# A three-block network on one core: row chains moved beside projections, narrow columns in one piece, eleven early expert picks

## What is computed (the reference, cut to what matters)

```
# block 1, end: product-key experts (peer); per token 8 heads x 16 picks = 128 experts
q = hb @ w_q                                   # 1024 -> 2048
s = q . sub_keys ; sub_s, sub_i = top_k(s, 16) # two half keys per head
top_s, top_i = top_k(sub_s0 + sub_s1, 16)      # 16 of 256 sums
act = gelu(hb . expert_u[expert]) * softmax(top_s)
out = sum over the 128 picks of act * expert_v[expert]
# block 2, two linear-attention branches in front of a scan over time
gla:  log_a = -softplus(-(lr @ w2 + b2)) / 16           ; cum = cumsum per chunk
hgrn: log_a = logaddexp(log lb, log(1-lb) + logsigmoid(f)); cum = cumsum per chunk
      k = (1 - lb) * sigmoid(-f) ; q = silu(q) * 128 ** -0.5
# block 3, two branches with one rate per head and token
mlstm: F = cumsum(logsigmoid(f + fb)) ; running maximum of i + ib - F
mamba: dt = softplus(dt + bias) ; cs = cumsum(-exp(a_log) * dt)
```

## Time and profile before

| | |
|---|---|
| median of 3 runs | 4499.88 (4499.08 to 4502.44) |
| profiled execution | 4488.02, span of the core 4486.3 |
| TensorE busy / VectorE busy | 83% / 65% of the span |
| ScalarE busy / GpSimd busy | 19% / 20% |
| granted TensorE clock, mean over the span | 0.943 |
| DMA | 900.51 MB, mean 201 GB/s, of which 656.07 MB in the software queue |

### The profile page before, as it was taken

How to read it: one execution, slowest core, us unless ns; L and a number is a source line. 1 busy time by engine, 2 the same in 40 slices (tenths; PEclk the granted TensorE clock), 3 DMA queues, 4 the chain that set the end, 5 groups by cost and what they waited for, 6 DMA issues and landing times. The chain is left out here.

```text
span 4486.3 us, 42942 instructions
## 1 busy us (share of the span) xinstructions
PE 3731.5 (83%) x15030; PEld 2541.7 (57%) x15030; DVE 2931.1 (65%) x5200; ACT 834.7 (19%) x1667; POOL 883.9 (20%) x810
## 2 busy tenths in 40 slices
PE   4999988778778777767999795959938997998987
PEld 3777774223222222225688685736726775777865
DVE  6653667787877878666555557638855546565774
ACT  1111111111111111111211225217721202311000
POOL 2010014344343434331000000025630000001001
PEclk8999999999999999998999897979968998999998
DMA  5523227999999999972234220339932131122321
GB/s 211 181 84 102 100 85 323 423 424 423 424 423 414 419 417 413 417 297 90 85 127 140 82 90 10 104 116 381 387 110 76 43 95 57 43 94 76 102 72 71
DMA packets 201760, 900.51 MB, mean 201 GB/s; under 512 B 21202, under 2 KB 23011, under 8 KB 122339
## 3 DMA queue, kind: packets, MB, share of 16 engines
q0 software_dynamic: 90448, 656.07, 35.9%
q1 hardware_dynamic: 105680, 230.81, 15.4%
q10 hardware_dynamic: 5428, 11.04, 0.7%
HBM read 869.03 MB, written 40.89 MB: 203 GB/s over the span
## 5 line engine op out<-in xcount | busy, mean ns | idle before, releaser
L123 DVE CAST ring_high<-ring_raw 128x2048 fp32r<-128x2048 f32 (+3 forms) x184 | 212.0, 1152 | 618.8 <-PE psum L153 521.5
L1395 PE MATMUL psum<-slots_ring,evacuation_tmp 128*128 128x512 f32 x816 | 404.2, 618 | 103.3 <-DVE evacuation_tmp L1489 102.7
L151 PE MATMUL psum<-ring_high,h_features 128*128 128x512 f32 x1120 | 452.8, 404 | 19.8 <-PEq L50 12.1
L153 PE MATMUL psum<-ring_high,h_features 128*128 128x512 f32 x1120 | 442.6, 395 | 0.0
L152 PE MATMUL psum<-ring_low,h_features 128*128 128x512 f32 x1120 | 442.5, 395 | 0.0
L125 DVE TENSOR_TENSOR ring_low<-ring_raw,ring_high 128x2048 fp32r<-128x2048 f32 (+3 forms) x184 | 394.6, 2144 | 15.2 <-issue 1.3
L151 PE MATMUL psum<-h_features,ring_high 128*128 128x512 f32 (+4 forms) x920 | 365.9, 398 | 30.9 <-DVE ring_low L125 17.3
L1395 PE MATMUL psum<-slots_features,evacuation_tmp 128*128 128x512 f32 x612 | 302.1, 617 | 78.2 <-DVE evacuation_tmp L1489 78.1
L152 PE MATMUL psum<-h_features,ring_high 128*128 128x512 f32 (+4 forms) x920 | 362.6, 394 | 0.0
L153 PE MATMUL psum<-h_features,ring_low 128*128 128x512 f32 (+4 forms) x920 | 362.0, 393 | 0.0
L1395 PEld LDWEIGHTS psum<-slots_ring,evacuation_tmp 128*128 128x128 f32 x816 | 138.2, 189 | 368.4 <-DVE evacuation_tmp L1489 269.3
(11 more groups left out here) (580 smaller groups left out, 6965.3 us busy)
## 6 DMA issues: line engine op xcount, KB each, us to landing
ring_raw<-in_w_in SPq DMA_DIRECT2D x94, 1024.0 KB, 5.2
ring_raw<-in_w_up_pairs SPq DMA_DIRECT2D x20, 1024.0 KB, 5.0
ada_ring<-in_w_ada POOLq DMA_DIRECT2D x16, 1024.0 KB, 5.7
ring_raw<-in_w_out SPq DMA_DIRECT2D x12, 1024.0 KB, 5.1
moe_entries<-in_const_zero_rows POOLq DMA_DIRECT2D x23, 512.0 KB, 4.1
row_room<-moe_entries SPq DMA_DIRECT2D x23, 512.0 KB
moe_results<-rows_out SPq DMA_DIRECT2D x23, 512.0 KB, 9.1
ring_raw<-in_w_down SPq DMA_DIRECT2D x10, 1024.0 KB, 4.9
```

Of the source, the lines that this page charges most:

```text
L123: nc.vector.tensor_copy(high, whole)
L151: nc.tensor.matmul(out, a[0], b[0], start=start, stop=False)
L153: return nc.tensor.matmul(out, a[1], b[0], start=False, stop=stop)
L1395: mm = nc.tensor.matmul(banks(t)[q], diagonal[:, n % DIAGONALS, :], slots[slot_of[n]][:, D + q * BANK:D + (q + 1) * BANK], start=i == 0, s ...
```

## The change

Five parts.

1. `peer`: 12 slots instead of 10 (two lie in the ring's raw places, so this stage no longer loads pieces for the next one; `norm` with rows does it instead). Eleven picks can be issued before `projected`: picks 0 to 2 at once, 3 when the last piece of half 0 is split, 4 to 6 into the slots of 0 to 2 when these were taken, 7 when the last piece of half 1 is split, 8 to 10 when TensorE has used the last half 0. VectorE makes the dot products of the first seven during the projection and adds them itself (`sum_early`), without TensorE. The key scores of a unit are issued one group after its projection, and the split pieces and routing steps are in another order.
2. GLA: the small matmul goes to the head of the `gdn_out` projection, and the rest of the chain beside it (`gla_decay`).
3. HGRN: bounds, sigmoid and silu go into the side of `gla_gates` (`hgrn_bound`), soft maxima and sums beside the `gla_out` projection (`hgrn_decay`).
4. mLSTM and Mamba: `mif` and `sdt` become one piece `few3` of 80 columns, projected first in `mlstm_in` as one group; both row chains run beside the rest of that projection (`rate_rows`). One stage (`turn_rows`) transposes all four rows. Mamba's chain is gone from its place.
5. `few` of block 2 becomes one piece of 80 columns and one group of 24 matmuls.

The diff, cut to its core:

```diff
+            if aside_pe is not None:
+                aside_pe(pe, lambda t: bank(1 - base % 2, t), *aside_sems)
...
+            if aside_pe is not None:
+                steps = aside_dve(lambda t: bank(1 - base % 2, t))(dve, *aside_sems)
+                advance(steps, 1)
+                dve.drain().then_inc(free[1 - base % 2], 1)
...
+            for _ in steps:
+                pass
...
+                load_ahead(core, sp, core.splits + 2)
...
-EARLY = 3
-SLOTS_UV = 10
+EARLY = 7
+EARLY_BATCHES = ((0, 3), (3, 7))
+SLOTS_UV = 12
+EARLY_ORDER = (0, 1, 2, 3, 0, 1, 2, 4, 5, 6, 7, 8, 9, 10, 11, 0, 1, 2, 3)
 DIAGONALS = 4
...
-                if n == EARLY:
+                if n == 3:
+                    pool.wait_ge(core.split[0], first + UNITS)
+                elif n == 7:
+                    pool.wait_ge(core.split[1], first + UNITS)
+                elif n == 8:
+                    pool.wait_ge(core.used, first + UNITS)
+                elif n == 11:
                     pool.wait_ge(projected, 1)
-                if n >= SLOTS_UV:
-                    pool.wait_ge(used_slot, n - SLOTS_UV + 1)
+                elif last_of[n] is not None and last_of[n] < EARLY:
+                    pool.wait_ge(taken_early, last_of[n] + 1)
+                elif last_of[n] is not None:
...
+            def sum_early(lo, hi):
+                dve.wait_ge(activated, hi)
+                own = slice(lo, hi)
+                nc.vector.tensor_tensor(weight[:, own], weight[:, own], gates[:, 0].rearrange("p h k -> p (h k)")[:, own], ALU.mult)
+                dve.drain()
+                for n in range(lo, hi):
+                    v = slots[slot_of[n]][:, D:2 * D]
+                    if n == 0:
+                        done = nc.vector.tensor_scalar(product_tmp, v, weight[:, n:n + 1], None, ALU.mult)
+                    else:
+                        done = nc.vector.scalar_tensor_tensor(product_tmp, v, weight[:, n:n + 1], product_tmp, ALU.mult, ALU.add)
+                    done.then_inc(taken_early, 1)
+                    dve.drain()
...
-            split_piece(nc, core, dve, first + 2, 0)
             router = route(0)
             advance(router, 10)
+            split_piece(nc, core, dve, first + 2, 0)
+            advance(router, Q)
             split_piece(nc, core, dve, first + 2, 1)
-            advance(router, 9)
-            split_piece(nc, core, dve, first + 3, 0)
-            advance(router, Q)
             router = route(1)
             advance(router, 10)
+            split_piece(nc, core, dve, first + 3, 0)
+            for n in range(*EARLY_BATCHES[0]):
+                dot(n)
+            advance(router, 3)
+            sum_early(*EARLY_BATCHES[0])
             split_piece(nc, core, dve, first + 3, 1)
+            advance(router, 7)
+            for n in range(*EARLY_BATCHES[1]):
+                dot(n)
             advance(router, Q)
-            for n in range(total_picks):
+            sum_early(*EARLY_BATCHES[1])
+            for n in range(EARLY, total_picks):
                 t, i = divmod(n, PICKS)
                 m = n // Q + LEAD
-                if n % Q == 0:
+                if n % Q == 0 or n == EARLY:
...
+def gla_decay(nc, core, lr, qkT, w2, b2, logs, last):
...
+    def act_part(act, gated, shifted, logged):
+        for u in range(2):
+            act.wait_ge(shifted, u + 1)
+            nc.scalar.activation(cum[:, u, :], logs[:, u, :], ACT.Abs)
+        act.drain()
+        nc.scalar.activation(cum[:, 0:2, :], cum[:, 0:2, :], ACT.Exp, scale=-1.0)
+        act.drain()
+        nc.scalar.activation(cum[:, 0:2, :], cum[:, 0:2, :], ACT.Ln, bias=1.0).then_inc(logged, 1)
+        yield
+    def dve_part(spare):
+        def part(dve, gated, shifted, logged):
+            for u in range(2):
+                dve.wait_ge(gated, u + 1)
+                nc.vector.tensor_scalar(logs[:, u, :], spare(u), b2[:, u:u + 1], -1.0, ALU.add, ALU.mult).then_inc(shifted, 1)
+            yield
+            nc.vector.tensor_scalar(qkT[:, 0:2, :], qkT[:, 0:2, :], 64 ** -0.5, None, ALU.mult)
+            yield
+            yield
+            yield
+            dve.wait_ge(logged, 1)
+            nc.vector.scalar_tensor_tensor(logs[:], logs[:], 0.0, cum[:, 0:2, :], ALU.max, ALU.add)
+            dve.drain()
+            nc.vector.tensor_scalar(logs[:], logs[:], -1.0 / 16.0, None, ALU.mult)
+            yield
+            dve.drain()
+            for u in range(2):
                 nc.vector.tensor_tensor_scan(cum[:, u, :], core.tile_row[:], logs[:, u, :], 0.0, ALU.mult, ALU.add)
             dve.drain()
-            for u in range(units):
+            for u in range(2):
                 nc.vector.tensor_copy(last[:, u, :], cum[:, u, :].rearrange("p (t n) -> p t n", t=NT)[:, :, P - 1])
...
+    def act_keys(act, come, differed, raised, bounded, logged, keyed):
+        act.wait_ge(come, 16 * number)
+        nc.scalar.activation(k[:], logs[:], ACT.Sigmoid, scale=-1.0).then_inc(keyed, 1)
+        yield
+        nc.scalar.activation(q[:], q[:], ACT.Silu).then_inc(keyed, 1)
+        yield
...
+    def dve_keys(dve, differed, raised, bounded, logged, keyed):
+        dve.wait_ge(keyed, 1)
+        for h in range(H):
+            nc.vector.tensor_scalar(k[:, h, :], k[:, h, :], lb[:, REST, h:h + 1], None, ALU.mult)
+        dve.wait_ge(keyed, 2)
+        nc.vector.tensor_scalar(q[:], q[:], 128 ** -0.5, None, ALU.mult)
+        yield
...
+def hgrn_decay(nc, core, logs, lb, last, tmp):
+    H = 4
+    def act_part(act, shifted, logged):
+        nc.scalar.activation(tmp[:], logs[:], ACT.Abs)
+        act.drain()
+        nc.scalar.activation(tmp[:], tmp[:], ACT.Exp, scale=-1.0)
+        act.drain()
+        nc.scalar.activation(tmp[:], tmp[:], ACT.Ln, bias=1.0).then_inc(logged, 1)
+        yield
+        for h in range(H):
+            act.wait_ge(shifted, h + 1)
+            nc.scalar.activation(tmp[:, h, :], logs[:, h, :], ACT.Abs, bias=lb[:, MINUS_LOG_LB, h:h + 1])
+        act.drain()
+        nc.scalar.activation(tmp[:], tmp[:], ACT.Exp, scale=-1.0)
+        act.drain()
+        nc.scalar.activation(tmp[:], tmp[:], ACT.Ln, bias=1.0).then_inc(logged, 1)
+        yield
+    def dve_part(dve, shifted, logged):
+        yield
+        yield
+        dve.wait_ge(logged, 1)
+        nc.vector.scalar_tensor_tensor(logs[:], logs[:], 0.0, tmp[:], ALU.min, ALU.subtract)
+        yield
+        dve.drain()
+        for h in range(H):
+            nc.vector.tensor_scalar(logs[:, h, :], logs[:, h, :], lb[:, LOG_REST, h:h + 1], None, ALU.add).then_inc(shifted, 1)
+        yield
+        yield
+        yield
+        yield
+        yield
+        dve.wait_ge(logged, 2)
+        for h in range(H):
+            nc.vector.scalar_tensor_tensor(logs[:, h, :], logs[:, h, :], lb[:, LOG_LB, h:h + 1], tmp[:, h, :], ALU.max, ALU.add)
+        dve.drain()
+        for h in range(H):
+            nc.vector.tensor_tensor_scan(logs[:, h, :], core.tile_row[:], logs[:, h, :], 0.0, ALU.mult, ALU.add)
+        dve.drain()
+        for h in range(H):
+            nc.vector.tensor_copy(last[:, h, :], logs[:, h, :].rearrange("p (t n) -> p t n", t=NT)[:, :, P - 1])
+        yield
+    return ("shifted", "logged"), None, dve_part, act_part, None
...
+    def dve_part(dve, rows_ready, shifted, logged, raised):
+        yield
+        yield
+        nc.vector.tensor_scalar(f_bias[:], f_bias[:], -1.0, None, ALU.mult)
+        nc.vector.memset(v[:, :, :, P:P + 1], 1.0)
+        dve.wait_ge(rows_ready, 1)
+        dve.drain()
+        nc.vector.tensor_scalar(f_row[:], f_row[:], -1.0, f_bias[:], ALU.mult, ALU.add).then_inc(shifted, 1)
+        nc.vector.tensor_scalar(dt_row, dt_row, 1.0, dt_bias[:], ALU.mult, ALU.add).then_inc(shifted, 1)
+        yield
+        yield
+        dve.wait_ge(logged, 2)
+        nc.vector.scalar_tensor_tensor(f_row[:], f_row[:], 0.0, sum_row[:], ALU.max, ALU.add)
+        nc.vector.scalar_tensor_tensor(dt_row, dt_row, 0.0, cs_row[:], ALU.max, ALU.add)
+        dve.drain()
+        nc.vector.tensor_tensor_scan(sum_row[:], core.one_row[0:H, :], f_row[:], 0.0, ALU.mult, ALU.add)
+        yield
+        nc.vector.tensor_scalar(cs_row[:], dt_row, a_rate[:], -1.0, ALU.mult, ALU.mult)
+        dve.drain()
+        nc.vector.scalar_tensor_tensor(i_row[:], i_row[:], i_bias[:], sum_row[:], ALU.add, ALU.add)
+        nc.vector.tensor_tensor_scan(cs_row[:], core.one_row[0:S_HEADS, :], cs_row[:], 0.0, ALU.mult, ALU.add)
+        dve.drain()
+        yield
+        nc.vector.tensor_tensor_scan(top_row[:], core.one_row[0:H, :], i_row[:], -3e38, ALU.mult, ALU.max)
+        dve.drain()
+        nc.vector.tensor_scalar(top_row[:], top_row[:], -1.0, None, ALU.mult)
+        dve.drain()
+        yield
+        nc.vector.tensor_tensor(sum_row[:], sum_row[:], top_row[:], ALU.add)
+        dve.drain().then_inc(raised, 1)
+        yield
+    return ("rows_ready", "shifted", "logged", "raised"), None, dve_part, act_part, None
...
```

(4 more changed lines are left out.)

449 lines of the change are left out of this document (240 added, 209 removed).

## The result

The changed kernel takes 4389.18 us in the median of four runs (4388.12 to 4396.54), the kernel before 4499.48 (4485.32 to 4502.44): ratio 0.9761, 95% interval 0.9739 to 0.9783. That is 110.3 us less; the forecast was 87.8 less, 4412, with a range from 4397. Between the two profiled executions it is 4488.02 against 4388.47, 99.5 us. Two executions of the kernel before in the sets further down took 5616.9 and 6478.7 us at a mean granted clock of 0.64 and 0.55; they are left out of all ranges and counts.

A forecast was written before the change was run, and what follows sets the result against it. Full DMA engines bound the gather loop; four chains of small VectorE and ScalarE instructions, 104.4 us, lay exposed. Terms summed to 87.8 us, taken from the median 4499.9 to give 4412, range 4397 to 4436.

The forecast's parts named there:

- peer: Gather loop: eleven picks instead of three before `projected`, eight gathers fewer at 2.496 us; 20.0 us less, bounds 8 and 27.
- GLA: Chain of 17.2 us ahead of the GLA scan goes beside the `gdn_out` projection; 11.3 us less, bounds 8 and 16.
- HGRN: Chain of 42.2 us ahead of the HGRN scan goes beside `gla_gates` and `gla_out`; 26.6 us less, bounds 15 and 34.
- mLSTM: Chain and narrow projection ahead of the mLSTM stage, 27.3 us, mostly go; 13.8 us less, bounds 5 and 22.
- Mamba: Chain of 17.7 us ahead of Mamba's scan goes, less a silu and a meeting; 16.1 us less, bounds 14 and 17.
- few: Projection delta_in: 48 matmuls fewer on TensorE, but VectorE's bound stays; 0 us gained, bounds 0 and 0.3.
- +6.8 of `few3`: Start of `mlstm_in`: 24 matmuls in front, partly at half clock, then TensorE waits for the first big piece; costs 6.8 us.
- rival B: Short stages could leave TensorE at full clock: up to 5 us at mLSTM, 2 to 3 elsewhere; 4403, chance 0.09.
- A: Query projection: VectorE's early picks come late, the last split delays it, half of peer's gain goes; 4425, chance 0.12.
- C: Gather loop: twelve slots absorb more of the loop's hiccups, 10 us more gained; 4401, chance 0.08.
- D: Work beside the `_out` projections is not hidden; GLA and HGRN keep lower bounds, 8 and 15; 4427, chance 0.10.
- E: Gather loop gets slower; a pace of 2.67 us per pick eats 88 us, 2.70 gives 4514; chance 0.03.

The follow-up runs named there:

- after_12: Changed kernel with one useless VectorE operation of 1024 columns, so its mLSTM stage starts 1.2 us later: 4405.5 us, ratio 0.9780.
- the new order: Kernel before with the mLSTM stage reordered, twelve full matmuls between a head's scores and its row and sums: 4496.6 us, ratio 0.9993.

## Why the prediction was wrong

Two steps failed. The clock stood in the sum at nothing, and the distance of 11.9 us between the profiled execution and the median was taken to be the same in both kernels. In the first pair of profiles what stood at nothing gave 11.7 us, 8.2 of them in the mLSTM and Mamba stages and the projection between them; the second step accounts for the other 10.8, by which the medians differ more than the two traces.

Differences between traces at the same instruction, for the first pair of profiles (4488.0 and 4388.5) and for the usual pair (4506.2 and 4390.3). Peer is read at the first split behind the gather loop, GLA from there to its scan, HGRN to its scan, mLSTM from the start of `mlstm_in` to the next stage's first split, Mamba from the last convolution to the first copy of its values:

| term | forecast | first pair | usual pair |
|---|---|---|---|
| peer | 20.0 | 19.3 | 18.3 |
| GLA | 11.3 | 10.8 | 11.0 |
| HGRN | 26.6 | 26.1 | 26.0 |
| mLSTM | 13.8 | 15.3 | 16.5 |
| Mamba | 16.1 | 16.3 | 16.3 |
| `few` | 0 | 0 | 0 |
| sum | 87.8 | 87.8 | 88.1 |
| all else | 0 | 11.7 | 27.8 |
| span | 87.8 | 99.5 | 115.9 |

**Right: every term of the working, within 2.7 us.** That the sum fits to 0.3 is partly luck, as peer gave less and mLSTM more. Pace 2.49, eleven issues, the last split 5 us ahead of need, 8.5 us behind gla_out's last evacuation (8.0 and 0.9), +2.4 in gla_gates: TensorE's gap before gla_out is 4.00 us instead of 1.54. (The prediction's own figures, 1.28 + 2.19 + 1.28 against 2.7, make 2.05, not 2.4; for the +6.8 of `few3` it shows no sum.) HGRN came out right by small errors against each other: the first eight matmuls behind that gap run at 1.2 GHz, 0.43 us apart instead of 0.23, which costs 1.6 that I had not counted, and the rest of the stage that much less. `few3` costs 7.8 in the usual pair (forecast 6.8), because the first wide piece is waited for, 5.85 us on the DMA; from there to the last v evacuation 1.0 is gained instead of 1.4 lost, and the chain gives 23.3 instead of 22.0. In delta_in the last narrow row now ends 1.5 us before VectorE's last split (2115.88 and 2117.34), which bounds the stage as before, and nothing is gained.

**Wrong: "The median of the runs is 11.9 above it; the same sum gives 4412".** I carried the distance between the profiled execution and the median over as if it were the same in both kernels; in the changed kernel it is 0.7 (4389.18 and 4388.47). It was a cost of 10 us in the mLSTM stage and some 8 behind it that the profiled execution of before happened to lack, in the very stretch that the change moves. The range failed with it: it took in the rivals one at a time, while the bounds of the terms, all at their upper end, add to 116. The view that could have warned me was the list of runs: 4485.3 was not among the first three, but 4488.0 beside 4499.1 to 4502.4 is no scatter.

**Wrong: the clock at nothing in the sum, and the size and the reason of rival B** (4403, chance 0.09). Its sign was right, its place too. But I took half clock to follow from the length of an idle gap, and priced it once per chain. In the usual pair 15.1 us are gained between the start of the mLSTM stage and the last convolution before Mamba (eight dips, two of them behind the stage, make 13 of it, the earlier rise most of the rest), 10.4 in Mamba's stage and 2.3 elsewhere; in the first pair 4.0, 4.2 and 3.4. The dips of the kernel before return round by round without any idle gap. The Trainium skill (TensorE: Matmul & The Clock Gate, "HAM oscillation — how this bites in real kernels") puts an oscillating clock down to TensorE's waits for data between bursts of matmuls. Here the traces differ: it is busy 3.00 of 3.00 us ahead of each fall, and the measurement decides.

**The gain is partly luck.** 88 us belong to the change. Of the rest, the part in the mLSTM stage depends on where the stage meets the clock: with 1.2 us more in front of it the six dips are there, and the median is 14 higher (`after_12`). An edit of 1.8 us on the kernel before won 12 without doing anything. Rivals A, C, D and E did not come: TensorE did not wait in the projection (ahead of the last piece), the pace stayed, and the work beside the `_out` projections cost what was counted.

What stays open: why the dips in Mamba's stage come in some executions (three in the first profile of before, none in the changed kernel's) was seen, not tested. That the break between 10.5 and 10.6 us is the true edge rests on one trace at either side, and what lies between 9.4 and 10.0 was not met. That the matmuls of 64 and 8 partitions bring the falls is argued from where the falls stand, from the last round without one, and from the new order, which also changed the rhythm of the heads; no run changed those matmuls alone.

## What to carry to other kernels

Read the distance between the profiled execution and the median as a term of the sum with a place of its own: profile the kernel twice, and if the runs fall on two levels, find the stage that makes them before counting anything. The mLSTM stage, in which TensorE alternates between full matmuls and ones of few partitions, won or lost 10% with a shift of 1 to 2 us ahead of it; so judge an edit of a few microseconds by its own rows, not by the time of the kernel. Counting chains instruction by instruction, with the engine that ends each stage, was good to 3 us a term.

## What the runs showed of the hardware

- The granted clock fell from 2.4 to 1.2 GHz while TensorE had no gap in the profile, six times in a row, 10.2 us apart, and each time behind the same matmuls (one head's scores, the next head's row); an undisturbed round takes 8.6 us. Each fall lasts 3.4 us and costs 1.6 to 1.7.
- Work on TensorE during an idle stretch did not protect what follows: 86 matmuls in 21 us of idle time, and the stage behind them was 10 us longer than without them (106.9 against 96.7; one trace each, and the medians are 15 us apart).
- A wait of TensorE of 4.00 us was followed by half clock for some 3 us (from 2644.1), one of 1.58 us by none.
